# Moving tiles staggered by 64 bytes and low weights moved by 512 bytes in SBUF, in a float32r matmul kernel of four residual sub-layers

## What is computed

```
for i in range(DEPTH):                       # DEPTH = 2
    hn = rmsnorm(x, mix_pre_g[i])
    y = pool_mixer(hn, ...) if i == 0 else mlstm_mixer(hn, ...)
    x = x + rmsnorm(y, mix_post_g[i])
    hn = rmsnorm(x, ffn_pre_g[i])
    a = relu(hn @ w1[i]);  y = (a * a) @ w2[i]   # 1024 -> 4096 -> 1024
    x = x + rmsnorm(y, ffn_post_g[i])
```

## Time and profile before

| | before |
|---|---|
| time, median of 3 runs | 1901.96 us (1899.02 to 1905.91) |
| time of the profiled execution | 1899.89 us |
| span of the profiled execution | 1898.1 us |
| PE busy | 1867.6 us (98%), 8526 matmul records |
| PE weight loads (PEld) busy | 1533.9 us (81%), 8526 |
| DVE busy | 1342.8 us (71%) |
| ACT busy | 1068.3 us (56%) |
| POOL busy | 89.8 us (5%) |
| mean DMA traffic | 150 GB/s |

### The profile page before, as it was taken

How to read it: one execution, slowest core, us unless ns; L and a number is a source line. 1 busy time by engine, 2 the same in 40 slices (tenths; PEclk the granted TensorE clock), 3 DMA queues, 4 the chain that set the end, 5 groups by cost and what they waited for, 6 DMA issues and landing times.

```text
span 1898.1 us, 24458 instructions
## 1 busy us (share of the span) xinstructions
PE 1867.6 (98%) x8526; PEld 1533.9 (81%) x8526; DVE 1342.8 (71%) x2120; ACT 1068.3 (56%) x1825; POOL 89.8 (5%) x121
## 2 busy tenths in 40 slices
PE   9999999999999999999999999999999999999999
PEld 6678888888888888888878888777888888888886
DVE  5877565655778987786866868777665656577885
ACT  7655555563445546766766757645655555445533
POOL 0110000000000200010000100021000000000010
PEclk9999999999999999999999999999999999999999
DMA  5344343448633533353323442245243436853353
GB/s 211 114 159 171 122 169 136 168 181 323 220 96 97 195 115 111 100 175 98 104 80 100 131 157 90 78 150 193 90 167 139 166 140 239 304 179 99 111 194 128
DMA packets 79706, 284.80 MB, mean 150 GB/s; under 512 B 9408, under 2 KB 9664, under 8 KB 71136
## 3 DMA queue, kind: packets, MB, share of 16 engines
q1 hardware_dynamic: 64288, 239.96, 36.1%
q0 software_dynamic: 8320, 27.27, 4.3%
q10 hardware_dynamic: 6976, 16.01, 2.7%
HBM read 211.31 MB, written 71.89 MB: 149 GB/s over the span
## 4 chain that ended last, share of the span: by engine, by line
PE 87%; DVE 8%; ACT 2%; issue 2%; DMA 0%; SPq 0%; DVEq 0%; ACTq 0%
PE core L1024 5%; PE core L1025 5%; PE core L1026 5%; PE bank L807 5%; PE bank L809 5%; PE bank L808 5%; PE core L974 5%; PE core L976 5%; PE core L975 5%; PE bank L1025 4%; PE bank L1024 4%; PE bank L1026 4%; PE bank L976 4%; PE bank L975 4%; PE bank L974 4%; PE bank L907 2%
## 5 line engine op out<-in xcount | busy, mean ns | idle before, releaser
L1471 ACT CAST h_hi<-h_raw 128x512 fp32r<-128x512 f32 x188 | 116.7, 621 | 230.9 <-PE core L1026 140.0
L1835 DVE TENSOR_TENSOR w_lo<-raw,w_hi 128x1024 fp32r<-128x1024 f32 x132 | 161.1, 1222 | 118.0 <-ACT w_hi L1285 115.9
L807 PE MATMUL bank<-x_hi,w_hi 128*128 128x512 f32 x560 | 224.4, 401 | 3.6 <-issue 2.9
L1285 ACT CAST w_hi<-raw 128x1024 fp32r<-128x1024 f32 x132 | 137.9, 1045 | 145.6 <-PE bank L809 45.4
L809 PE MATMUL bank<-x_hi,w_lo 128*128 128x512 f32 x560 | 218.5, 390 | 0.0
L808 PE MATMUL bank<-x_lo,w_hi 128*128 128x512 f32 x560 | 218.2, 390 | 0.0
L2092 DVE TENSOR_TENSOR h_lo<-h_raw,h_hi 128x512 fp32r<-128x512 f32 x188 | 129.5, 689 | 109.6 <-ACT h_hi L1471 109.6
L1024 PE MATMUL core<-h_hi,w_hi 128*128 128x512 f32 x464 | 180.9, 390 | 1.7 <-DVE y L2158 1.6
L1026 PE MATMUL core<-h_hi,w_lo 128*128 128x512 f32 x464 | 180.5, 389 | 0.0
L1025 PE MATMUL core<-h_lo,w_hi 128*128 128x512 f32 x464 | 180.5, 389 | 0.0
L1986 DVE TENSOR_TENSOR w_lo<-sums,w_hi 128x512 fp32r<-128x512 f32 x104 | 71.7, 689 | 96.4 <-ACT w_hi L1313 93.6
(11 more groups left out here) (334 smaller groups left out, 4375.5 us busy)
## 6 DMA issues: line engine op xcount, KB each, us to landing
raw<-weights SPq DMA_DIRECT2D x132, 512.0 KB, 3.3
h_pair_dram<-y SPq DMA_DIRECT2D x26, 1792.0 KB, 6.6
h_raw<-h_pair_dram SPq DMA_DIRECT2D x182, 256.0 KB, 2.8
w<-second_pairs SPq DMA_DIRECT2D x24, 768.0 KB, 4.5
raw_odd<-first_pairs SPq DMA_DIRECT2D x14, 1024.0 KB, 7.1
x_scratch<-y POOLq DMA_DIRECT2D x48, 256.0 KB, 2.5
raw<-first_pairs SPq DMA_DIRECT2D x12, 1024.0 KB, 7.1
xold<-x_scratch POOLq DMA_DIRECT2D x40, 256.0 KB, 3.3
```

What stands on the lines that cost most here:

```text
L807: nc.tensor.matmul(o, a, hi(t), start=(k == 0), stop=False)
L1285: nc.scalar.copy(w_hi[:, ROW[u] * T:(ROW[u] + 2) * T], raw[:, (n % RAW) * BLK:(n % RAW + 1) * BLK]).then_inc(hi_ready, 1)
L1835: dve.tensor_tensor(w_lo[:, s], raw[:, (n % RAW) * BLK:(n % RAW + 1) * BLK], w_hi[:, s].bitcast(F32), ALU.subtract).then_inc(lo_ready, 1)
```

## The change

The change touches only the placement of tensors. It adds dummy tensors: 512 bytes between `w_hi` and `w_lo`, and 64 bytes (`LINE` = 16 float32 values) between and behind the high and low tensors of all seven quadrants. Two placeholders that keep overlapping arenas in step grow by the same 14 lines.

```
+LINE = 16
...
         w_hi = sb("w_hi", [P, ROWS * T], F32R)
+        sb("w_apart", [P, P])
         w_lo = sb("w_lo", [P, ROWS * T], F32R)
...
             for q in ("11", "21", "22", "12"):
                 XQ_HI[q] = sb1(f"x{q}_hi", [P, 4, T], F32R)
+                sb1(f"x{q}_apart", [P, LINE])
                 XQ_LO[q] = sb1(f"x{q}_lo", [P, 4, T], F32R)
+                sb1(f"x{q}_behind", [P, LINE])
...
                 for q in ("t1", "t3", "t2"):
                     XQ_HI[q] = top.enter_context(nc.sbuf_tensor(f"x{q}_hi", [P, 4, T], F32R))
+                    top.enter_context(nc.sbuf_tensor(f"x{q}_apart", [P, LINE], F32))
                     XQ_LO[q] = top.enter_context(nc.sbuf_tensor(f"x{q}_lo", [P, 4, T], F32R))
+                    top.enter_context(nc.sbuf_tensor(f"x{q}_behind", [P, LINE], F32))
...
-            arena.enter_context(nc.sbuf_tensor("not_used", [P, 6 * T], F32))
+            arena.enter_context(nc.sbuf_tensor("not_used", [P, 6 * T + 14 * LINE], F32))
...
-            behind.enter_context(nc.sbuf_tensor("all_arenas", [P, 4 * PAIRS * T + (2 * H_RING + 6 + H_RAW) * T], F32))
+            behind.enter_context(nc.sbuf_tensor("all_arenas", [P, 4 * PAIRS * T + (2 * H_RING + 6 + H_RAW) * T + 14 * LINE], F32))
```

## The result

The changed kernel takes 1915.64 us (median of 6 runs, 1914.26 to 1918.83) against 1901.92 us of the kernel before (6 runs, 1899.02 to 1905.91). The ratio is 1.0073, with a 95% interval of 1.006 to 1.0087: 13.7 us more. The time lies inside the range given, but in the case that had a chance of 0.16, not in the likeliest one.

What follows compares the result with a forecast made beforehand. The prediction took TensorE's pace to bound the kernel and every term as 0, so 1898.1 + 0 = 1898.1 us; between the profiled time and the run median 1901.96 it chose 1901 us, range 1891 to 1921.

Steps and rivals of the forecast that it cites:

- What bounds the kernel: Whole kernel: TensorE, busy 1867.6 of 1898.1 us; only its own pace or a new wait of it can move the time.
- The counts: Full-rate matmuls whose moving start shifts: 4440 with x and xt, 2400 with h, together 6840.
- C's second price: If crossing a 2,048-byte border slows h too: 6840 matmuls at 4.4 ns, 30 us, time 1931.
- I take 0 for the stagger: Moving tiles: stagger and border crossing cost 0, since rows that differ in address do not differ in time.
- the bound: Per full-rate matmul: a gain of at most 10.3 ns; for a loss, the 231 ns pace behind a pause, 4.4 ns more.
- my comparison in the earlier trace: Plain float32 products: kT at 1280, crossing a block, 0.85 us; x_last at 0, 0.86; so crossing costs under 5 ns each.
- at half the rate: Plain float32 products: 430 ns a record, taken as moving data read at half rate, only 3 ns lost between two records.
- The rows on weights: Second MLP product: weights at 0, 512, 1024, 1536 against h_hi at 0 all give 227 ns; moving w_lo costs 0.
- Rival B: Matmuls with x and xt: stagger frees reads from one shared bank; up to 46 us faster, 1855, or 1878; chance 0.14.
- no change: Whole kernel, likeliest case: interaction depends on when the streams read, not where; 1901 us, within 1895 to 1907; chance 0.70.
- Rival C: Matmuls with x and xt: 64-byte alternation, 16 columns out of phase, keeps 231 ns; 19.5 us slower, 1921; chance 0.16.
- The rule of independent ports: TensorE's SBUF reads: moving operand and weight load have own ports, PE never waits; so nothing changes, sum 0.

Runs made afterwards that it cites:

- w_lo_512: Against the kernel before: only w_lo and all that stands behind it moved by 512 bytes, no moving tile staggered; 1901.4 us, ratio 0.9993.
- quadrants_64: Against the kernel before: high and low tile of a quadrant begin at the same offset, each quadrant 64 bytes further than the last; 1914.58 us, ratio 1.0062.
- apart_256: Against the kernel before: x_lo begins 256 bytes past x_hi in the four x quadrants, t quadrants not staggered; 1901.86 us, ratio 0.9997.
- all_64: Against the kernel before: all moving tiles, x, xt and h alike, begin 64 bytes further against the weights; 1913.29 us, ratio 1.0056.
- both_32: Against the kernel before: weights and moving tiles moved together by 32 bytes; 1903.69 us, ratio 1.0003.
- weights_16: Against the kernel before: both weight rings begin 16 bytes later, all moving tiles stay; 1934.73 us, ratio 1.0169.
- pairs_w128: Against the kernel before: seven quadrants with seven different pairs of high and low starts, w_lo 128 bytes past w_hi; one run, 1927.86 us.

## Why the prediction was wrong

**What bounds the kernel** was right: the whole change of time is one of TensorE's pace, with DVE, ACT and the weight loads busy as long as before.

**The counts** were right where they mattered: the 4440 matmuls with x and xt slowed, the others did not. "Together 6840" leaves out 744 float32r matmuls (early_h, hp and hid); the program has 7584. That touches only the 30 us of C's second price.

**The step that failed** is "I take 0 for the stagger", drawn from plain float32 products, which take 430 ns a record for one load of weights. I wrote myself that "these rows have slack that full-rate reads lack", and then let them outweigh the bound. At full rate a distance of 64, 128 or 192 in all passes costs 2.3 to 6.4 ns (229.0 to 233.1 against 226.7), and the change's own two patterns cost 4.5 and 5.2 ns (231.2 and 231.9). A second flaw sits in my comparison in the earlier trace rows: kT at 1280 against `ones` at 0 is distance 0 modulo 256, x_last at 0 against `consts` at 832 is 192. The pair differs in two things at once, so it could not price the crossing. That the crossing is free was right, but by luck; w_lo_512 shows it. What the pair does show is that these products do not feel a distance of 192. That they read "at half the rate" is my reading of the 430 ns; whether the columns come slowly or twice, no run shows.

**The rows on weights** The earlier trace rows were read rightly as far as they go. They varied the distance in steps of 512, two periods, so they could not show anything finer. Rival B said exactly this of a possible gain ("those rows do not exclude it"); it is as true of a loss. All distances of before were at the one place that turned out to be the best of those tried, so any dependence could only show as a loss. With no full-rate row at another distance, 0.70 for "no change" was too much.

**Rival C** had the sign, the size and the place: 4.4 ns for each of 4440 matmuls, 19.5 us, 1921. Measured are 4.6 ns (231.6 against 227.0, the mean over all matmuls with x and xt without pauses), which makes 20.4 us. PE busy rose by 18.0; matmuls behind pauses, which ran at 231 ns already before, may be part of the difference. The span rose by 14.4, since 3.6 us came out of PE's idle time, which fell from 30.5 to 26.9 us. That term I left out; it is most of why the result lies 5 us under C. Of its mechanism, half holds. Alternation is not needed (quadrants_64 lost as much without it), and one of 256 bytes costs nothing (apart_256), which "16 columns out of phase" does not foresee. But an alternation of 64 bytes does add: x11, x22, t1 and t2 of the change run at 231.9 ns, slower than at 64 bytes throughout. C's reason, a phase that never settles, was not tested.

**Rival B** is excluded for every arrangement tried. The far end of its price, 3 ns instead of 13.3 lost per matmul, was never approached. What those 13.3 ns at distance 0 are made of stays open: no run here takes away the weight load or the full read rate.

**The rule of independent ports.** The Trainium skill, SBUF — State Buffer, section "Who interferes with whom", says that the moving operand and the weight load have independent ports and that PE never waits on anyone. The measured pace decides against "nothing changes": in all_64, with the same instructions, a distance of 64 bytes costs 2.3 ns per matmul, and in both_32 a common shift of 32 bytes costs none. So the pace depends on where the two reads of TensorE stand to each other. That they meet in banks which repeat every 256 bytes is a guess; the runs show the period, not the banks, and no run takes one of the two reads away.

## What to carry to other kernels

When TensorE is the bound and streams float32r at full rate, count its records in a stretch without idle time: 226.7 ns for 512 columns is the best pace seen here, and a steady 229 to 234 ns without any wait points at placement. In a kernel like this one, let all moving tiles and weights, high and low parts alike, begin at the same place modulo 256 bytes; aligning to 2,048 is not needed, and pads put in to spread addresses should be multiples of 256. And if a trace holds only one value of the quantity that a change varies, a neighbouring case with slack is no evidence for "no effect": give both signs more room.

## What the runs showed of the hardware that was not expected

- The pace of full-rate float32r matmuls depends on the distance between moving tile and weights modulo 256 bytes: 226.7 ns at 0, 229.0 to 230.1 at 64, 232.6 to 234.3 at 32, 96, 128, 160, 192 and 224, 233.3 in the second product with weights 16 bytes further (weights_16).
- It depends on alternation between the passes as well, unless that is a multiple of 256 bytes: 231.9 ns with x_lo alone 64 bytes further (after), and 231.6 ns in the product with x11 of pairs_w128, though each moving tile there stands at distance 0 to the weights loaded while it streams.
- Moving both by 32 bytes changes nothing (ratio 1.0003), nor does a tile that crosses a 2,048-byte border (w_lo_512, ratio 0.9993).
- Shifting only w_lo, used by one pass in three, by 64, 128 or 192 bytes costs the same each time, 231.1 ns on average (736 records in 170 us).
- Plain float32 products with operands at distances 0 and 192 modulo 256 take the same time.
